# A hybrid attention layer: masks and position biases added by VectorE instead of TensorE, and convolution taps earlier

## What is computed

```python
def sliding_window_gqa(q, k, v, sinks, bias_tab):          # 8 heads, 2 key heads
    logits = einsum(q, k) * HEAD_DIM ** -0.5
    bias = bias_tab[rel_bucket(dist)]                      # depends on query - key only
    logits = where(mask, logits + bias, NEG)
    ...                                                    # softmax with a sink, times v
def forgetting_attention(q, k, v, f_logit, b_f):           # 8 heads
    logits = einsum(q, k) * HEAD_DIM ** -0.5 + c_query - c_key
    logits = where(kpos <= qpos, logits, NEG)              # c: running sums of log sigmoid
def moba_attention(q, k, v, bias_tab):                     # 8 heads; one block of 256 here
    lo = einsum(q, k) * scale + bt[:, rel_bucket(dist)]
    lo = where(dist >= 0, lo, NEG)
```

## Time and profile before

| | |
|---|---|
| Median of 3 runs | 1834.34 us (1834.06 to 1834.34) |
| Profiled execution, its own time | 1833.8 us |
| Its span | 1832.0 us |
| Mean granted TensorE clock | 0.976 |
| First score product, last head done | 142.85 us, 330.75 us |

### The profile page before, as it was taken

One profiled execution on the slowest core, in us unless ns is written; L12 is line 12 of the kernel. 1 busy time (PEld: TensorE's weight loads), 2 busy tenths in 40 slices (PEclk: granted clock), 3 DMA queues, 4 the chain that ended last, 5 costly groups with the idle time before them and its releaser, 6 DMA issues.

```text
span 1832.0 us, 22946 instructions
## 1 busy us (share of the span) xinstructions
PE 1654.3 (90%) x9878; PEld 1045.4 (57%) x9878; DVE 735.9 (40%) x1260; ACT 486.7 (27%) x818; POOL 151.5 (8%) x186
## 2 busy tenths in 40 slices
PE   6999999988999999898999988888888888888885
PEld 5998888888999888897433332323232222323221
DVE  5667754576986376655312121211111111212122
ACT  4344454445554344452211010100000000001001
POOL 1200000230553003001000000000000000000000
PEclk8999999999999999999999999999999999999998
DMA  7653322444665442565699999999999999999995
GB/s 200 185 185 112 99 89 92 140 160 136 186 185 184 161 151 85 172 216 205 266 418 423 424 424 422 424 425 423 423 423 425 423 425 423 425 424 424 423 425 228
DMA packets 209386, 525.98 MB, mean 287 GB/s; under 512 B 18073, under 2 KB 134734, under 8 KB 176510
## 3 DMA queue, kind: packets, MB, share of 16 engines
q1 hardware_dynamic: 206830, 519.62, 73.5%
q0 software_dynamic: 2448, 4.82, 1.1%
HBM read 523.31 MB, written 1.07 MB: 286 GB/s over the span
## 4 chain that ended last, share of the span: by engine, by line
PE 42%; DMA 31%; DVE 3%; ACT 1%; issue 0%; SPq 0%; ACTq 0%; DVEq 0%
PE bank L593 41%; DMA slot_ring<-in_w_down 10%; DMA slot_memx<-in_w_down 7%; DMA slot_high<-in_w_down 5%; DMA slot_late<-in_w_down 5%; DMA slot_ring<-in_w_gu 1%; DMA slot_high<-in_w_gu 1%; DMA slot_last<-in_w_gu 1%; DMA slot_late<-in_w_gu 1%; PE bank L1076 1%; DVE rot_tmp L2178 0%; DVE x_sb L1811 0%; DVE slot_ring_r L1803 0%; ACT L1412 0%; DVE rstd L1842 0%
## 5 line engine op out<-in xcount | busy, mean ns | idle before, releaser
L593 PE MATMUL bank<-h_hi_r,high_r 128*128 128x256 f32 x1000 | 287.8, 288 | 9.1 <-DVE slot_ring_r L1803 9.1
L593 PE MATMUL bank<-h_lo_r,high_r 128*128 128x256 f32 x1000 | 285.1, 285 | 0.0
L1803 DVE TENSOR_TENSOR slot_ring_r<-slot_ring,high_r 128x1024 fp32r<-128x1024 f32 x198 | 243.5, 1272 | 99.3 <-ACT high_r L1412 99.2
L593 PE MATMUL bank<-h_hi_r,slot_ring_r 128*128 128x256 f32 x952 | 271.5, 285 | 0.0
L1807 DVE TENSOR_SCALAR ga<-bank 128x512 f32<-128x512 f32 x32 | 22.1, 692 | 584.1 <-PE bank L593 584.1
L1412 ACT ACTIVATE high_r<-slot_ring 128x1024 fp32r<-128x1024 f32 x198 | 197.9, 1053 | 64.1 <-PE bank L593 49.5
L593 PEld LDWEIGHTS bank<-h_hi_r,high_r 128*128 128x128 f32 x1000 | 193.9, 194 | 9.9 <-DVE slot_ring_r L1803 9.8
L593 PEld LDWEIGHTS bank<-h_lo_r,high_r 128*128 128x128 f32 x1000 | 194.1, 194 | 0.1
L1412 ACT ACTIVATE th_e<-ga 128x512 f32<-128x512 f32 x32 | 20.2, 630 | 619.6 <-DVE ga L1807 619.6
L593 PEld LDWEIGHTS bank<-h_hi_r,slot_ring_r 128*128 128x128 f32 x952 | 184.4, 194 | 0.0
L593 PE MATMUL bank<-slot_ring,xg 128*64 128x512 f32 x528 | 125.1, 605 | 12.4 <-DMA slot_ring<-in_w_gu 12.4
(11 more groups left out here) (410 smaller groups left out, 2958.5 us busy)
## 6 DMA issues: line engine op xcount, KB each, us to landing
slot_ring<-in_w_gu SPq DMA_DIRECT2D x66, 1024.0 KB, 22.0
slot_high<-in_w_gu SPq DMA_DIRECT2D x50, 1024.0 KB, 22.2
slot_ring<-in_w_down SPq DMA_DIRECT2D x49, 1024.0 KB, 21.3
slot_last<-in_w_gu SPq DMA_DIRECT2D x38, 1024.0 KB, 22.2
slot_ring<-in_w_in SPq DMA_DIRECT2D x36, 1024.0 KB, 5.0
slot_late<-in_w_gu SPq DMA_DIRECT2D x32, 1024.0 KB, 22.2
slot_high<-in_w_down SPq DMA_DIRECT2D x25, 1024.0 KB, 22.7
slot_ring<-in_w_up SPq DMA_DIRECT2D x44, 512.0 KB, 4.6
```

The costliest lines, as they stand in the source:

```text
L593: return e.matmul(o, lhs, rhs, start=start, stop=stop, skip_group_check=True)
L1803: return e.tensor_tensor(o, i, j, op)
```

## The change

TensorE's products with `flip` and with the causal mask are gone. VectorE adds bias or mask while it moves the scores from the bank to `score`, takes the maxima there, and works on the kinds in an interleaved order; ScalarE makes the exponentials in place. To have the rows in the order of the queries, `diag_dram` holds every head's diagonal 128 times, and the tile is read with a step of 383, beginning at value 127. Six more convolution steps stand ahead of the loop over heads; inside it they start at 13.

```diff
-        diag_dram = nc.dram_tensor("diag_dram", (BIAS_H, TOEP), F32).ap()
+        diag_dram = nc.dram_tensor("diag_dram", (BIAS_H, P, TOEP), F32).ap()
...
                 if kind == "swa":
                     qt, kt = qa[r, pair, :], ka[r, :]
-                    q.wait_ge(*toep_in[2 * n % 8]["toep", 2 * n])
...
-                for c, qs, ks, cs in ((PARTS[0], slice(128, 256), slice(0, 256), slice(0, 256)),
-                                      (PARTS[1], slice(0, 128), slice(0, 128), slice(128, 256))):
-                    matmul(b[:, c], qt[:, qs], kt[:, ks], True, False)
+                for c, qs, ks in ((PARTS[0], slice(128, 256), slice(0, 256)), (PARTS[1], slice(0, 128), slice(0, 128))):
+                    m = matmul(b[:, c], qt[:, qs], kt[:, ks], True, kind != "fox")
                     if kind == "fox":
-                        matmul(b[:, c], fox_pair(fox_l, n)[:, qs], fox_pair(fox_rt, n)[:, ks], False, False)
-                        m = matmul(b[:, c], ident, C("causal")[:, cs], False, True)
-                    else:
-                        m = matmul(b[:, c], C("flip"), toep[(2 * n + (kind == "moba")) % 8][:, cs], False, True)
+                        m = matmul(b[:, c], fox_pair(fox_l, n)[:, qs], fox_pair(fox_rt, n)[:, ks], False, True)
                 m.then_inc(*pe.step(*name))
-                banks.give(name, (act, ("exp", kind, n)))
+                banks.give(name, (dve, ("biased", kind, n)))
...
-                e.dma_start(diag_dram[i * SWA_H:(i + 1) * SWA_H, :], diag_sb[i]).then_inc(*diag_out.step("diag"))
+                e.dma_start(diag_dram[i * SWA_H:(i + 1) * SWA_H, :, :],
+                            diag_sb[i].rearrange("h (o m) -> h o m", o=1).broadcast_to([SWA_H, P, TOEP])).then_inc(*diag_out.step("diag"))
...
                 if n >= 8:
-                    q.wait_ge(*pe["scores", kind, n // 2 - 4])
-                src = bass.AP(diag_dram.tensor, head * TOEP, [[1, P], [1, S]])
+                    q.wait_ge(*dve["biased", kind, n // 2 - 4])
+                src = bass.AP(diag_dram.tensor, head * P * TOEP + P - 1, [[TOEP - 1, P], [1, S]])
...
             def exponents(kind, n):
-                b, st = bank(("scores", kind, n)), stat_of(kind, n)
+                st = stat_of(kind, n)
                 q.wait_ge(*dve["maxima", kind, n])
-                if n:
-                    q.wait_ge(*pe["probs", kind, n - 1])
                 for i, c in enumerate(PARTS):
-                    af(score[kind][:, c], b[:, c], ACT.Exp, bias=st[:, i:i + 1], accum_out=st[:, 2 + i:3 + i]).then_inc(
+                    af(score[kind][:, c], score[kind][:, c], ACT.Exp, bias=st[:, i:i + 1], accum_out=st[:, 2 + i:3 + i]).then_inc(
                         *act.step("exp", kind, n))
...
             for i in range(2):
                 ahead(("qa", i))
-                if i == 0:
-                    conv_step(0)
+                conv_step(i)
...
-            conv_step(1)
+            conv_step(2)
             ahead(("ka", 0))
             evac(("ka",), ka, bank(("ka", 0))[:, 0:S], ("ka", 0))
-            conv_step(2)
+            conv_step(3)
+            conv_step(4)
             for g, (k, kt) in enumerate((("d", kd), ("c", kc))):
                 for i in range(2):
                     ahead(("q" + k, i))
+                    conv_step(5 + 2 * (2 * g + i))
                     ahead(("k" + k, i))
                     evac(("k" + k, i), kt[:, 2 * i:2 * i + 2, :], two_of(("k" + k, i)), ("k" + k, i))
                     ahead(("v" + k, i))
-                    conv_step(3 + 2 * g + i)
-
-
-            def softmax(kind, n):
-                b, st, sc = bank(("scores", kind, n)), stat_of(kind, n), score[kind]
-                nm, sm = st[:, 0:2], st[:, 2:4]
+                    conv_step(6 + 2 * (2 * g + i))
+
+
+            def maxima(kind, n):
+
+                b, nm, sc = bank(("scores", kind, n)), stat_of(kind, n)[:, 0:2], score[kind]
+                i = 2 * n + (kind == "moba")
+                if kind != "fox":
+                    q.wait_ge(*toep_in[i % 8]["toep", i])
+                added = C("causal") if kind == "fox" else toep[i % 8]
                 q.wait_ge(*pe["scores", kind, n])
+                if n:
+                    q.wait_ge(*pe["probs", kind, n - 1])
+                for c, cs in zip(PARTS, (slice(0, 256), slice(128, 256))):
+                    tt(sc[:, c], b[:, c], added[:, cs], ALU.add).then_inc(*dve.step("biased", kind, n))
+                own()
                 for i, c in enumerate(PARTS):
-                    e.tensor_reduce(nm[:, i:i + 1], b[:, c], AX.X, ALU.max, negate=True).then_inc(*dve.step("maxima", kind, n))
+                    e.tensor_reduce(nm[:, i:i + 1], sc[:, c], AX.X, ALU.max, negate=True).then_inc(*dve.step("maxima", kind, n))
...
             for n in range(8):
-                for kind in KINDS:
-                    softmax(kind, n)
+                maxima(KINDS[0], n)
+                maxima(KINDS[1], n)
+                normalise(KINDS[0], n)
+                maxima(KINDS[2], n)
+                normalise(KINDS[1], n)
+                normalise(KINDS[2], n)
                 ahead(("gz", 2 * n))
-                conv_step(7 + 3 * n)
+                conv_step(13 + 3 * n)
                 ahead(("gz", 2 * n + 1))
-                conv_step(8 + 3 * n)
+                conv_step(14 + 3 * n)
...
-                conv_step(9 + 3 * n)
+                conv_step(15 + 3 * n)
```

More of the change, by code:

```diff
@@ L65, in shape_constants @@
     parts["ident"] = np.eye(P)
-    parts["flip"] = np.eye(P)[::-1]
     parts["tri"] = (i[:, None] < i[None, :])
@@ L732, in scores @@
                     q.wait_ge(*dve["kd", 1])
-                    q.wait_ge(*toep_in[(2 * n + 1) % 8]["toep", 2 * n + 1])
                 else:
@@ L792, in tensor_program @@
                 project(("gz", 2 * n), hs, h_of("ln1_g"), (act, ("gz", 2 * n)))
-                conv_norm(7 + 3 * n)
+                conv_norm(13 + 3 * n)
                 for kind in KINDS:
@@ L796, in tensor_program @@
                 project(("gz", 2 * n + 1), hs, h_of("ln1_g"), (act, ("gz", 2 * n + 1)))
-                conv_norm(8 + 3 * n)
+                conv_norm(14 + 3 * n)
                 for kind in KINDS:
                     values(kind, n)
-                conv_norm(9 + 3 * n)
+                conv_norm(15 + 3 * n)
             pe.mark("attention end")
@@ L1952, in vector_program, with normalise @@
                     ahead(("v" + k, i))
-                    conv_step(3 + 2 * g + i)
-            def softmax(kind, n):
-                b, st, sc = bank(("scores", kind, n)), stat_of(kind, n), score[kind]
-                nm, sm = st[:, 0:2], st[:, 2:4]
-                q.wait_ge(*pe["scores", kind, n])
+                    conv_step(6 + 2 * (2 * g + i))
[5 more added lines that the diff above has]
+                added = C("causal") if kind == "fox" else toep[i % 8]
+                q.wait_ge(*pe["scores", kind, n])
+                if n:
[3 more added lines that the diff above has]
+                own()
                 for i, c in enumerate(PARTS):
-                    e.tensor_reduce(nm[:, i:i + 1], b[:, c], AX.X, ALU.max, negate=True).then_inc(*dve.step("maxima", kind, n))
+                    e.tensor_reduce(nm[:, i:i + 1], sc[:, c], AX.X, ALU.max, negate=True).then_inc(*dve.step("maxima", kind, n))
                 if kind == "swa":
-                    head = head_of(kind, n)
                     own()
-                    ts(nm, nm, neg_sinks[:, head:head + 1], ALU.min).then_inc(*dve.step("maxima", kind, n))
+                    ts(nm, nm, neg_sinks[:, head_of(kind, n):head_of(kind, n) + 1], ALU.min).then_inc(*dve.step("maxima", kind, n))
+            def normalise(kind, n):
+                st, sc = stat_of(kind, n), score[kind]
+                sm = st[:, 2:4]
+                if kind == "swa":
                     q.wait_ge(*act["sink exp", n])
```

## The result

The changed kernel takes 1853.51 us (median; 1851.72 to 1856.95), the kernel before 1834.34: the ratio is 1.0112, 95% interval 1.0093 to 1.0131. It is slower, by 19 us, and I had forecast 10. The profiled execution has a span of 1852.9 us, 20.9 above the one of before.

A forecast was written before the change was run, and what follows sets the result against it. TensorE was taken to bound the kernel, busy for 90% of the span. 1833.8 - 25.0 - 10 + 0.5 + 0.7 + 45 = 1845, taken as 1844 us for overlap; 1834 to 1854 for this case, 1798 to 1854 overall.

The forecast's parts named there:

- the split of the forget weights: Ahead of attention, VectorE's second convolution step delays this split: TensorE starts 0.7 us later, plus 1 us after the stall.
- Products removed, -25.0: In attention, mask and bias products of three kinds in eight rounds vanish from TensorE, 1.04 us each: 25.0 us gained.
- Granted clock, -10: In attention, denser TensorE work keeps the clock whole in rounds that lost 11 us: 10 us gained, ends 0 and 11.
- fourth rival: In attention the clock falls as before: 10 us more on any case; no chance of its own.
- VectorE, +0.5: In attention, additions and new order leave VectorE late only for the second round's probabilities, mostly covered: 0.5 us lost.
- third rival: VectorE bounds the attention rounds after all: 1855 to 1865 us with the stall, about 1815 without; no chance of its own.
- The writing, 61 us: Ahead of attention, writing 3.15 MB of diagonals out of 8 partitions at 52 GB/s lasts from 28.6 to about 90 us.
- first rival: Diagonal copies go at engine rate, 16 us, or do not hold engines: stall 0 to 2 us, total 1802; chance 0.26.
- the second: Rival: the diagonal writing takes 32 us, to 61; TensorE starts the query unit at 64.5: +16, total 1815; chance 0.11.
- The stall, 42.5 us to 93: Ahead of attention, slow writing delays the first query unit's weights: TensorE starts it at 93, not 50.6, 42.5 us lost.
- so SP gets about 1.6 packets for each of GpSimd's: On the DMA engines during the writing, SP's queue gets at most 181 turns by 90 us, holding back the query unit.
- The clock behind it, +2: After the 42 us rest for the query unit, TensorE begins at 1.2 GHz: about 2 us lost.

The follow-up runs named there:

- e7: e1 with maxima and normalisation of one kind after the other, as in the kernel before, not interleaved: 1819.01 us.
- e4: The kernel before without its 48 mask and bias products and with nothing in their place, so scores go unmasked: 1806.47 us.
- e6: e1 with all convolution taps where the kernel before had them, three steps in each of the first three attention rounds: 1805.30 us.
- e5: e1 with the second step of convolution taps put back behind the forget gate: 1799.81 us.
- e11: The changed kernel, 128 copies kept, with only the second step of convolution taps put back behind the forget gate: 1848.82 us.
- e1: The changed kernel with 23 copies of each diagonal in memory in place of 128, read over two strides: 1804.66 us.
- e9: The changed kernel with its writing cut into 16 transfers, one per diagonal, each read out of one partition: 1880.79 us in one run.
- e3: The changed kernel writing the same 3.15 MB out of 128 partitions of constants in 16 transfers, true diagonals left out: 1797.79 us.
- e2: The kernel before with only the writing changed, every diagonal written 128 times as in the changed kernel: 1880.56 us.
- e8: The changed kernel with 65 copies of each diagonal (1.6 MB) in place of 128: 1824.25 us.
- e10: The changed kernel with each diagonal written to memory once, then copied 128 times from memory to memory by one transfer: 1805.75 us.

## Why the prediction was wrong

The sign, the main mechanism and its place held; the size did not: +19.2 us measured, +9.7 forecast. The step that failed is the split of the forget weights: priced at 0.7 + 1 us, with nothing for the clock behind it, it took 4.5 and 2.6 us. That is 5.4 of the 9.5 us missing. By its own terms:

- **Products removed, -25.0.** Too small: -29.9. A round's scores shrink by 3.74 us (142.85 to 149.98, now 198.21 to 201.60), not 3.12. I priced only the products that go. Those that stay also start sooner: the two of one kind with 64 rows in a row take 0.76 and 0.65 us together, where they had stood 0.62 + 0.42 apart among products of 128 rows.
- **Granted clock, -10.** Too large: about -6, the rest of the 35.8 with the small terms. Above 17.95 the rounds still lose 1.6 us three times (4.9, where before lost 11). The fourth rival, the clock as before, was half right; my argument from the first round held for every other round. The two errors cancel in attention, which is luck.
- **VectorE, +0.5.** As small as forecast, partly by luck: nothing waits there, because the interleaving is worth 14 us (e7), where I had valued it at three waits of about 1 us in the rounds with taps. The additions measure 418 and 281 ns, as expected, and no wait stands between them and the maxima. The third rival is out for the changed kernel; e4 and e6 show that it was near.
- **The split of the forget weights, +0.7, and "1 us more" in the stall.** The failed step. TensorE waits 5.5 us there instead of 1.1, and then the clock falls: 0.51 around the end of that rest, for which the sum had nothing and which cost 2.3 us at the forget gate and 0.3 behind it. Taking the step away gives back 4.9 and 4.7 us (e5, e11). I had let VectorE begin the step at its old time, when it had 2.46 us of slack ahead of the forget split. But now the first taps, a split and the step run without a gap from 106.98 to 115.7, behind units that come late together, and TensorE is through with its products at 110.45. It does not take the long stall: with the writing down to 12 us, where ScalarE waits 5.8 us at most for a query unit, the wait is still 4.9 (e1).
- **The writing, 61 us.** Right: 60.3, by the row of the burst, which was one row of 0.24 us, so some luck is in it. The first rival, at engine rate, and the second, 32 us, are out. The time goes by the partitions that are read and not by the bytes: some 90, 60 and 12 us for 1, 8 and 128 partitions a transfer (e9, the changed kernel and e3). The Trainium skill, "SBUF — State Buffer", Door 1, ties the rate to the number of ports that the partitions reach; the prediction's estimate from it, 58 us, agrees with the 60.3.
- **The stall, 42.5 us to 93.** Nearly right: 43.7, and 96.92 because this execution began 2.5 us late. Its step "so SP gets about 1.6 packets for each of GpSimd's" did fail: from 35.4 to 89.5 us SP had 432 packets beside 760, 0.57 for each. So the query unit had nearly all of its packets to come when the writing ended. But from then on SP's queue had the engines nearly to itself (1.25 MB from 89.5 to 95 us), so the error cost little more than 1 us.
- **The clock behind it, +2.** Right: 2.0 us up to the second query unit, at 0.65 for the first 6 us.

Ahead of attention I had 46.2 us before rounding (42.5, 2, and 0.7 + 1 for the split) and 55.4 came. The 9.2 more are, within rounding, 1.2 of the stall, 2.8 at the forget gate, 2.6 of the clock behind it, and 2.5 of the late beginning, which is in this profiled execution; whether the median of the runs holds it too is not known. Attention gave back 1.3 more than forecast, and the sum had been rounded down by 1.

## What to carry to other kernels

Here a broadcast that read the same few partitions many times cost by its source, not by its bytes, and it took the engines away from every queue: look at where a transfer reads before calling it small, and let a second stride, or one copy in memory, do the multiplying. On an engine with slack the order of a dependent chain can matter more than its load: ask when the last link is ready, not how long the engine works. A step that is free in its own place is not free ahead of a small split that the bounding engine waits for, above all if everything there is already late. And before two traces are subtracted, look whether they begin alike: 2.5 us of this difference stood there ahead of anything that was changed.

## What the runs showed of the hardware

- Out of 8 partitions 3.15 MB took 60 us, out of 128 some 12, out of memory 14; cut into 16 transfers of one partition each they took some 90 (36 GB/s at 94% of the engines' time between 50 and 60 us, where the changed kernel has 56). A packet of the changed kernel held its engine 1.07 us, one from 128 partitions 0.14; both are worked out from the share of the engines' time.
- While such packets were under way TensorE stood 13.3, 13.8, 11.4 and 12.8 us (changed kernel, e2, e8, e11) for "issue" in the midst of a unit whose weights were there. The traces point at its instructions. On the queue that the profile calls instruction (q8) the first packet after 28 us comes at 62.8, 61.5, 61.4 and 60.5 in these four, and TensorE runs again 2.2 to 2.4 us later each time; in the kernel before that packet comes at 32.6, and in e9, with the longest writing and no such wait, at 44.9; e1, e3 and e10 have no such wait either. For which engine a packet is, the profile does not say, and no run tried it. From 62.5 to 63.0 us in the changed kernel:

```profile
q8 instruction: 1, 0.02, 11.6%
```

- Two products with 64 rows each, one behind the other, take 0.65 to 0.76 us for 384 columns; between products with 128 rows they stand for 1.04.
- In attention the clock alternates from the second round on, 1.00 in one round and 0.91 in the next, in the changed kernel and in e1. What sets that is open.
- The same 16 products at 10.8 us took 3.72 us in some executions and 5.5 to 6.2 in others (changed kernel, e5, e7, e8, e9, e10), at a granted clock of 1.00 in the record of both. What decides it is open.
